# Compression products in f32 from early loaded weights, in one row behind the value projection; compression bias transfers on GpSimd's queue

## The reference

```
h = rmsnorm(x, norm_mix); proj = h @ w_in          # queries, keys, values, gates g_a, g_b
blocks = kv[:, idx] + pos                           # 31 blocks x 2 groups, each 32 tokens x 64
k_cmp, v_cmp = gelu(blocks @ w1) @ w2               # w1: 2048 x 256, one for keys, one for values
y_a = window attention, y_b = compressed + selected + window attention
merged = sigmoid(g_a) * (y_a @ w_up_a) + sigmoid(g_b) * (y_b @ w_up_b)
x = x + merged @ w_out; then a convolved feed-forward, a second block, a last norm
```

## Time and profile before

| | |
|---|---|
| median of 3 runs | 1109.83 us (1109.31 to 1114.26) |
| profiled execution, its own time | 1111.78 us |
| its span | 1110.0 us |
| TensorE products, busy | 1054.4 us (95%), 5118 |
| TensorE weight loads, busy | 874.7 us (79%) |
| VectorE / ScalarE / GpSimd busy | 627.6 / 563.5 / 445.8 us |
| mean granted clock of TensorE | 0.982 |
| DMA | 111.87 MB, mean 101 GB/s |
| GpSimd low halves (L638) | 155, mean 2429 ns |
| ScalarE high halves (L696) | 162, mean 1058 ns |

### The profile page before, as it was taken

One profiled execution on the slowest core, in us unless ns is written; L12 is line 12 of the kernel. 1 busy time (PEld: TensorE's weight loads), 2 busy tenths in 40 slices (PEclk: granted clock), 3 DMA queues, 4 the chain that ended last, 5 costly groups with the idle time before them and its releaser, 6 DMA issues.

```text
span 1110.0 us, 15249 instructions
## 1 busy us (share of the span) xinstructions
PE 1054.4 (95%) x5118; PEld 874.7 (79%) x5118; DVE 627.6 (57%) x1415; ACT 563.5 (51%) x1154; POOL 445.8 (40%) x215
## 2 busy tenths in 40 slices
PE   6999889999999999999999999999999989889798
PEld 4888778899888778888888888778887778666577
DVE  4536556888835466554545455442235988586732
ACT  5443667777724344444444444443244263887821
POOL 1444552343424443444444444414444244443323
PEclk9999999999999999999999999999999999898999
DMA  5364442111013332222223223243252122343213
GB/s 198 95 175 135 132 148 76 50 47 39 30 38 133 123 104 95 95 95 94 97 94 109 95 96 133 95 141 106 98 187 103 59 88 93 100 109 86 76 49 113
DMA packets 40604, 111.87 MB, mean 101 GB/s; under 512 B 7219, under 2 KB 10419, under 8 KB 39859
## 3 DMA queue, kind: packets, MB, share of 16 engines
q1 hardware_dynamic: 29724, 91.80, 25.3%
q10 hardware_dynamic: 10824, 19.35, 5.5%
HBM read 100.25 MB, written 7.96 MB: 97 GB/s over the span
## 4 chain that ended last, share of the span: by engine, by line
issue 44%; PE 26%; POOL 15%; DVE 8%; ACT 3%; DMA 1%; SPq 1%; POOLq 1%; ACTq 0%; DVEq 0%
POOL WLO L638 13%; PE PS L1816 6%; PE PS L1818 6%; PE PS L1817 6%; PE PS L1998 2%; PE PS L2021 2%; PE PS L1957 1%; PE PS L1958 1%; DVE PB L1326 1%; DMA X<-xT 1%; PE PS L2160 1%; ACT PB L879 1%; DVE BLO L1239 1%; DVE PB L1364 1%; ACT WHI L696 1%
## 5 line engine op out<-in xcount | busy, mean ns | idle before, releaser
L638 POOL TENSOR_TENSOR WLO<-RAW,WHI 128x1024 fp32r<-128x1024 f32 x155 | 376.4, 2429 | 542.7 <-ACT WHI L696 542.5
L696 ACT ACTIVATE WHI<-RAW 128x1024 fp32r<-128x1024 f32 x162 | 171.2, 1058 | 291.6 <-PE PS L1818 260.2
L1816 PE MATMUL PS<-HHI,WHI 128*128 128x512 f32 x648 | 257.4, 397 | 12.7 <-DVE HLO L1217 9.0
L1817 PE MATMUL PS<-HLO,WHI 128*128 128x512 f32 x648 | 255.0, 394 | 0.0
L1818 PE MATMUL PS<-HHI,WLO 128*128 128x512 f32 x648 | 254.6, 393 | 0.0
L1816 PEld LDWEIGHTS PS<-HHI,WHI 128*128 128x128 f32 x648 | 123.4, 190 | 41.1 <-issue 11.5
L1816 PE MATMUL PS<-BHI,WHI 128*128 128x512 f32 x368 | 145.2, 395 | 3.2 <-POOL WLO L638 1.8
L1818 PEld LDWEIGHTS PS<-HHI,WLO 128*128 128x128 f32 x648 | 123.4, 190 | 26.3
L1818 PE MATMUL PS<-BHI,WLO 128*128 128x512 f32 x368 | 143.4, 390 | 0.0
L1817 PE MATMUL PS<-BLO,WHI 128*128 128x512 f32 x368 | 143.3, 389 | 0.0
L1817 PEld LDWEIGHTS PS<-HLO,WHI 128*128 128x128 f32 x648 | 123.3, 190 | 25.3 <-issue 0.5
(11 more groups left out here) (316 smaller groups left out, 1675.7 us busy)
## 6 DMA issues: line engine op xcount, KB each, us to landing
RAW<-wstream SPq DMA_DIRECT2D x162, 512.0 KB, 3.2
X<-xT ACTq DMA_DIRECT2D x4, 512.0 KB, 9.5
bias_b<-bias_rows ACTq DMA_DIRECT2D x2, 1024.0 KB
FX<-bias_b ACTq DMA_DIRECT2D x8, 256.0 KB, 2.8
X<-xT ACTq DMA_DIRECT2D x8, 256.0 KB, 3.7
x_keep<-X ACTq DMA_DIRECT2D x2, 1024.0 KB, 6.0
X<-x_keep ACTq DMA_DIRECT2D x2, 1024.0 KB, 5.1
outT<-X ACTq DMA_DIRECT2D x8, 256.0 KB, 2.5
```

The source lines that it names most:

```text
L638: pool.tensor_tensor(WLO[:, s, :], RAW[:, s, :], WHI[:, s, :].bitcast(F), ALU.subtract).then_inc(split_lo, 1)
L696: act.activation(WHI[:, c % 2, :], RAW[:, c % 2, :], ACT.Copy).then_inc(split_hi, 1)
L1816: pe.matmul(dst, a[0], b[0], start=first, stop=False, **kw)
L1817: pe.matmul(dst, a[0], b[1], start=False, stop=False, **kw)
```

## The change

- The eight compression units leave the stream. Their weights are loaded as they are, by four transfers of 1 MB on GpSimd's queue ahead of the low halves of units 2 to 5, into the tiles that held the split blocks (`w1_at`, over the high and low tiles of `CB`).
- The blocks aren't split. They are built in `X` (`CBX`, free between the first norm and the gates), one array for keys and one for values; VectorE clears these in the projection loop (c = 5 and 6).
- `compress` issues 4 unsplit f32 products of 256 columns instead of 12 split ones per call, 32 in all, in one row behind the value projection. The first gate units follow behind the first scores (`TAIL` from -2); step 2 has no unit.
- The activation comes ahead of the first exponentials; transposes, `w2` and the placing come in steps 0, 1 and 2 instead of 3, 4 and 5.
- The eight spreads of the compression bias go to GpSimd's queue (one ahead of each low half of units 8 to 15), and so do the eight loads behind them (two ahead of each of units 16 to 19), with a wait for the spreads between.
- ScalarE loses the conversions of blocks and units, the spreads and the loads; VectorE the low halves of the blocks. The numbers of later units fall by 8; where they lie in DRAM doesn't change.

```diff
-AHEAD = [("ga", 0), ("cmp", 0), ("ga", 1), ("cmp", 1)]
-FILL = {2: [("cmp", 7)], 3: [("ga", 4)], 4: [("ga", 5)]}
-TAIL = {-1: [("ga", 2), ("cmp", 2)], 0: [("cmp", 3), ("ga", 3), ("cmp", 4)], 1: [("cmp", 5), ("cmp", 6)], 5: [("ga", 6)], 6: [("ga", 7)]}
+FILL = {3: [4], 4: [5]}
+TAIL = {-2: [0], -1: [1], 0: [2], 1: [3], 5: [6], 6: [7]}
...
-GA_BANK = [3, 1] + [5] * 6
+GA_BANK = [3] + [5] * 7
...
+        def w1_at(w, half):
+            return (BF, BG)[half][:, CB[w]:CB[w] + 4, :].rearrange("p a b -> p (a b)")
+
+        CBX = [X[:, 4 - 4 * w:8 - 4 * w, :].rearrange("p a b -> p (a b)") for w in (0, 1)]
...
# GpSimd
-            at = 2
+            at = UNIT["proj"] + 2
+            for j in range(4):
+                w, half = divmod(j, 2)
+                pool.dma_start(w1_at(w, half).rearrange("p (u c) -> p u c", u=2),
+                               t["wstream"][17 + 2 * j:19 + 2 * j].rearrange("u p c -> p u c")).then_inc(ld_w1[w], 16)
+                low_halves(at, at + 1)
+                at += 1
+            low_halves(at, UNIT["proj"] + 8)
+            at = UNIT["proj"] + 8
+            pool.wait_ge(st_rows, 16)
+            for pg in range(8):
+                src = bass.AP(tb_dram.tensor, 8 * OH + OH_A + OH_B + 15 * CMP_A + 9 - pg,
+                              [[OH, NH], [-CMP_A, 16], [1, CMP_W]])
+                pool.dma_start(bias_c[:, 16 * pg:16 * pg + 16, :], src).then_inc(spread_c, 16)
+                low_halves(at, at + 1)
+                at += 1
+            pool.wait_ge(spread_c, 16 * 8)
+            for h in range(NH):
+                pool.dma_start(BCMP[:, h, :], bias_c[h]).then_inc(ld_cmp, 16)
+                if h % 2:
+                    low_halves(at, at + 1)
+                    at += 1
...
# ScalarE
-                if c in (9, 10):
-                    for pg in range(4 * (c - 9), 4 * (c - 9) + 4):
...
-                        act.dma_start(bias_c[:, 16 * pg:16 * pg + 16, :], src).then_inc(spread, 16)
...
-            def blocks_high(w):
...
-            u = UNIT["gc"]
-            for c in range(len(AHEAD)):
...
-                for h in (2 * c, 2 * c + 1):
-                    act.dma_start(BCMP[:, h, :], bias_c[h]).then_inc(ld_cmp, 16)
...
+            act.wait_ge(spread, 16 * 4)
+            bias_load(0)
+            bias_load(1)
+            act.wait_ge(cmp_done, 8)
+            act.activation(FX[:, 6, :], PS[:, 2, :], ACT.Gelu_apprx_tanh).then_inc(gelu_done, 1)
...
# VectorE
             for c in range(11):
+                if c in (5, 6):
+                    link(dve.memset(X[:, 4 * (c - 5):4 * (c - 4), :], 0.0))
...
-            link(dve.memset(PB[:, 0:2048], 0.0))
...
             blocks(0)
-            blocks_low(0)
-            dve.wait_ge(cb_lo, 1)
             blocks(1)
...
# TensorE
-                pe.wait_ge(cb_lo, w + 1)
-                arrive(c)
-                cbs = [cat(x, CB[w], 4) for x in (0, 1)]
+                pe.wait_ge(cb_built, w + 1)
+                pe.wait_ge(ld_w1[w], 32)
+                w1 = w1_at(w, n % 4 // 2)
                 for j in range(4):
                     tp = 4 * (n % 4) + j
-                    ins = three(PS[:, 2, 256 * w:256 * w + 256], [b[:, tp * P:(tp + 1) * P] for b in cbs],
-                                weight(c, j, 256, 256), tp == 0, tp == 15)
-                ins.then_inc(unit_used, 1)
+                    o = 1024 * (n % 2) + 256 * j
+                    ins = pe.matmul(PS[:, 2, 256 * w:256 * w + 256], CBX[w][:, tp * P:(tp + 1) * P], w1[:, o:o + 256],
+                                    start=tp == 0, stop=tp == 15)
+                ins.then_inc(cmp_done, 1)
...
             pe.wait_ge(proj_out, 13)
-            for kind, n in AHEAD:
-                gc(kind, n)
+            for n in range(8):
+                compress(n)
```

More of the change, by code:

```diff
@@ L68, in tail, with ga_unit @@
     return UNIT["tail"] + TAIL_UNITS.index(name)
-def gc_unit(kind, n):
-    return UNIT["gc"] + GC.index((kind, n))
+def ga_unit(n):
+    return UNIT["gc"] + n
 def ua_bank(n):
@@ L138, in build @@
         BHI = sb("BHI", [P, 24, SEQ], R)
+        with nc.sbuf_tensor("BG", [P, 24, SEQ], F) as BG:
+            pass
         BLO = sb("BLO", [P, 24, SEQ], R)
@@ L216, in build @@
         ga_done, ga_sig, ua_half, ua_done, ld_xr = [sem(s) for s in ("ga_done", "ga_sig", "ua_half", "ua_done", "ld_xr")]
-        spread, mem_sq = sem("spread"), sem("mem_sq")
+        spread, spread_c, mem_sq = sem("spread"), sem("spread_c"), sem("mem_sq")
         mem_hi, mem_lo, mem_acc, mem_rows, mem_tot, mem_rin, mem_rstd = [sem("mem_" + s) for s in
@@ L540, in _ @@
                 elif c < UNIT["ua"]:
-                    kind, n = GC[c - UNIT["gc"]]
-                    src = w[17 + n] if kind == "cmp" else w[25 + 3 * n]
+                    src = w[25 + 3 * (c - UNIT["gc"])]
                 elif c < UNIT["merge"]:
@@ L605, in _ @@
             for c in range(UNIT["tail"] // 2 * 2, NPOS):
-                at = c - 4 if c < UNIT["tail"] else c - 2
+                at = c + 4 if c < UNIT["tail"] else c + 6
                 if UNIT["tail"] <= c < UNIT["wout2"]:
                     name = TAIL_UNITS[c - UNIT["tail"]]
-                    at = UNIT["tail"] + STORED.index("ukv" if name[:2] == "uk" else name)
+                    at = UNIT["tail"] + 8 + STORED.index("ukv" if name[:2] == "uk" else name)
                 sp.wait_ge(split_lo, c - 1)
@@ L842, in attention @@
                             act.wait_ge(A["pv"], m["n"] - 2)
-                        if name == "ab" and i - 1 == 0:
-                            used(gc_unit("cmp", 3))
                         if name == "ab" and i - 1 == 1:
                             act.wait_ge(A["pv"], 1)
-                        if name == "ab" and i - 1 == 2:
-                            used(gc_unit("cmp", 7))
                         pt = turned_slot(name, m)
@@ L855, in attention @@
                             ins.then_inc(A["p_hi"], 1)
-                    if name == "ab" and i == LAST_CMP + 2:
+                    if name == "ab" and i == 1:
                         act.wait_ge(gelu_t, 1)
                         act.activation(FX[:, 7, :], PS[:, 2, :], ACT.Copy).then_inc(gelu_copied, 1)
-                    if name == "ab" and i == LAST_CMP + 3:
+                    if name == "ab" and i == 2:
                         act.wait_ge(cmp_mm, 1)
@@ L899, in attention @@
                         for u in fills(i - 1):
-                            stream(gc_unit(*u) + 2)
-                    if name == "ab" and i == LAST_CMP + 1:
-                        act.activation(FX[:, 6, :], PS[:, 2, :], ACT.Gelu_apprx_tanh).then_inc(gelu_done, 1)
+                            stream(ga_unit(u) + 2)
                     if name == "ab" and UA_FILL.get(i - 1, 0) % 2:
@@ L1409, in attention @@
                     if name == "ab":
-                        for kind, n in fills(i - 1):
-                            if kind == "ga":
-                                gate_a(n, gc_unit("ga", n))
+                        for n in fills(i - 1):
+                            gate_a(n, ga_unit(n))
                     if name == "ab" and i == LATE_K:
@@ L1920, in compressed @@
             def compressed(step):
-                if step == LAST_CMP + 1:
+                if step == 0:
                     pe.wait_ge(gelu_done, 1)
@@ L2061, in attention @@
                         for u in FILL.get(i, []):
-                            gc(*u)
-                    if name == "ab" and i in (LAST_CMP + 1, LAST_CMP + 2):
+                            gate_a(u)
+                    if name == "ab" and i in (0, 1):
                         compressed(i)
```

59 lines of the change are left out of this document (15 added, 44 removed).

## The result

The changed kernel took 1103.44 us (median of 5 runs, 1101.44 to 1104.12) beside 1111.11 us for the kernel before on the same chip: ratio 0.9927, 95% interval 0.9911 to 0.9943, 7.7 us or 0.7% less. The forecast was 1102.6 us in a range of 1099 to 1110, from a kernel before at 1109.83.

The account below looks back on a forecast made before the run. The prediction took TensorE to bound the kernel nearly everywhere, with its loose stage at the compression units. Gains 6.84 + 1.70 + 2.7 + 1.23 = 12.5 less costs 2.3 + 2.5 + 0.5 = 5.3 gave 7.2 us: 1102.6 us, range 1099 to 1110.

Parts of the forecast that it names:

- Part 1: Compression units: taking their weights out of the stream removes six TensorE stalls behind GpSimd's low halves, a gain of 6.84 us.
- Part 2: Gate unit behind the longest compression stall: 7.17 us at the low clock falls to 5.47, a gain of 1.70 us.
- part 5: ScalarE's and GpSimd's queues: 1.23 us gained before the value projection, 0.5 lost ahead of unit 16, early weights priced at nothing.
- the sum: Whole kernel: gains of 12.5 us less costs of 5.3 us, net 7.2 us, giving 1102.6 us.
- the early stall: TensorE's wait until 92.05, behind ScalarE's late conversion: goes when the bias spreads leave ScalarE's queue, a gain of 1.23 us.
- Part 3: Window map steps: 2.7 us of TensorE's waits for VectorE displaced, 2.5 us of new ones in steps 2 and 3.
- Part 4: Compression products on TensorE: 32 f32 products add 13.7 us, the split ones removed save 11.4, net cost 2.3 us.
- rival B: Row of f32 products: the clock falls to 1.2 GHz there, costing 11.9 us, 1114.5 us in all; chance 0.09.
- rival C: GpSimd's queue: DMA issues cost 4 us each and delay value and projection units, 1118.7 us; chance 0.05.
- Rival A: Window maps: later steps wait 5 us on VectorE and ScalarE, GpSimd's issues cost 2 us, 1106.6 us; chance 0.22.
- Rival D: Compression stage: it does not bound and TensorE's time is regained later, leaving 1109.8 us; chance 0.07.

Follow-up runs that it names:

- the three sets: The unaltered changed kernel timed three times beside the kernel before: 1103.44, 1102.07 and 1103.04 us, ratios 0.9927, 0.9915 and 0.9916.
- the second bias late: Changed kernel with the second attention bias's two 1 MB spreads moved on ScalarE's queue to behind the value projection: 1101.67 us, ratio 0.9915.
- late weights: Changed kernel with the four 1 MB compression weight loads issued ahead of units 8, 10, 12, 14 instead of 2 to 5: 1107.68 us, ratio 0.9965.

## Why the prediction was right

By its own steps:

- **Part 1, the stalls.** Right. Six stalls of the earlier trace rows are absent, and the kernel with the bias transfers alone, which left the compression in the stream, has five with 6.1 us. 6.84 us was the largest term of the sum. No run keeps the split products and loads their weights early, so what the early loads and what the unsplit products give by themselves was not measured apart.
- **Part 2, the low clock.** Right for the one stretch: the gate unit is at 5.46 us, 7.17 before. What the prediction did not count is a second slow stretch of this profile of before, clock 0.97 from 165.41 to 219.90, 1.6 us. That and the 0.5 us of part 5 that weren't spent account, with 0.4 us over, for the 7.7 us that the stage gave where the sum without the early stall says 12.5 - 1.23 - 5.3 = 6.0. It is at 0.50 from 209 to 212, behind a wait for VectorE of 0.84 us at 207.04; the changed kernel has that wait too (0.82 us at 201.90) and passes it at full clock. So these 1.6 of the stage's 7.7 us are more likely luck than the change. Such a second stretch comes and goes. The bias transfers moved alone have one behind their stall at 160.67 (0.68 from 160 to 165), the three profiles of the changed kernel have none, but three variants with the same schedule have one behind the VectorE wait of step 2 (0.86 and 0.80 around 165 with the bias back on ScalarE, 0.81 and 0.85 with the second bias late, 0.66 from 165 to 170 with late weights), and their stages are 121.8, 121.7 and 122.4. How much of it the change takes away for good is open.
- **Part 3, VectorE.** Right. 2.7 us displaced against 2.5 new was a net of -0.2; the sums of waits say +0.2 (3.8 and 4.0 us). The new waits are where they were put, around the scores of map 5 and the transposes of map 3, 159.69 and 162.52. One of 0.60 us at 205.43 was not forecast; the kernel with the bias transfers alone has it too.
- **Part 4, the products.** 13.7 us forecast, 13.62 in the timeline, 13.8 by doubling the row. The price per column from four late records held for 64. The clock held too, so rival B is refuted. Its evidence was no sign for this row, and not even a steady one: in the changed kernel's first profile the product behind the same 33 x 16 f32 products takes

```profile
16.93 3.66 PE L1850 MATMUL PS<-FX,TBL 33*16 33x416 f32 x10
20.52 0.50 PE L1803 MATMUL PS<-HHI,WHI 128*128 128x512 f32 x1
```

  and the clock is full there, where the earlier trace rows had 0.65 us. In that execution it fell 7 us later, behind an idle time. In six of the twelve profiles, before among them, it does fall between 20 and 22 us, at the end of these small products or just behind it; what decides between the two places is open.
- **Part 5, the queues.** The 1.23 us stall went and came back with the transfers on ScalarE: right. GpSimd's issues, bounded by nothing and 1.7 us, are 0.55 to 0.94, so rival C is refuted and the 0.5 us ahead of unit 16 were not spent. The price of nothing for 4 MB of early transfers held as far as the profiles can tell: the streamed loads between 45 and 92 us take as long in the kernel before (median 5.8, longest 9.2 us) as in the third profile of the changed one (6.0 and 8.9). What the prediction missed is that these loads come late in both kernels, beside the bias spreads: it took 3.2 us and allowed for twice that, and the longest take 9 to 10. Where the kernel before has 0.24 us for it, the changed kernel has 0.8 to 1.0, and that takes back about half of what the 1.23 us gave. Whether this difference is the change's or chance is not shown.
- **Rival A.** Given back to VectorE: not here. Shown possible by the gate unit moved to step 2, where 2 to 4 us went that way.
- **Rival D.** Refuted: the rest of the span is 886 to 890 us in every profile, before and after, and hands the stage's gain on.
- **The sum.** Net 7.2 us forecast; 7.7, 9.0 and 8.4 us between the medians of the three sets. The forecast time came closer than its parts: it started from 1109.83 us, where later medians of the kernel before are 1110.9 to 1111.5, and the gain was 0.5 to 1.8 us larger than forecast. One miss makes the forecast time too low and the other too high. The span of the profiled execution, 1101.4 us for a forecast 1102.8, is partly luck as well: its 8.6 us less are 7.7 in the stage, 3.1 in the rest and -2.2 ahead of the stage, and the last two are of the size by which executions of one program differ.

## What to carry to other kernels

A unit of streamed weights that gives TensorE less work than its refill takes costs a stall and then slow products behind it; taking it out of the stream pays even if its products become dearer (here 2.3 us more work for 8.5 us of stalls and low clock). Load such weights where the stream has not yet become tight: the same 4 MB were free when issued between 18 and 42 us and cost 4.2 to 5.6 us when issued between 57 and 96, beside the bias spreads. Before costing a gap in one profile, profile the same program again and cut the span in stages; here the early part moved by 2.8 us and the rest by 2.8 us with nothing changed, while the stage of the change held to 0.1 in the three profiles of the changed kernel. Even that is no bound: variants with the same order of work in the stage gave up to 122.4 us for its 120.

## What the runs showed of the hardware

- DMA issues on GpSimd stand in its own timeline and take time there: 0.94 us for the first of 1 MB and 0.74 to 0.75 for the next, 0.61 to 0.68 for a spread of 28 KB, 0.55 for a plain load. On ScalarE's queue three of the same spreads took 5.07 us.
- An f32 product of 256 columns with 128 x 128 weights takes two records of 0.213 us, 1.67 ns a column, the same in a row of 32 and in one of 64, at a granted clock of 1.00.
- Beside two spreads of 512 KB in rows of 1 KB the landing of a 512 KB streamed load went from 3.2 to as much as 10.9 us.
- At the start of this kernel the clock falls once, to 0.50, in each of the twelve profiles, but between 20 and 22 us in six of them and between 28 and 30 in the other six; of the three executions of the changed kernel two are of the first kind and one of the second. In the early ones no idle time stands ahead of the fall. In the late ones 1.73 to 1.75 us of idle time do, which otherwise lie behind slow products.
